# One core, one hybrid layer and a mixture-of-experts block: the conditioning rows gathered in one PSUM bank, and the order of Grams and transpositions in the RWKV pairs

## What is computed

```python
c_act = jax.nn.silu(c)
mod = c_act @ w_mod[l] + b_mod[l]
sh1, sc1, gt1, sh2, sc2, gt2 = [m[:, None, :] for m in jnp.split(mod, 6, axis=-1)]
```

```python
def step(S, inp):
    r_t, w_t, k_t, v_t, a_t, b_t = inp
    sa = jnp.einsum("bhij,bhj->bhi", S, a_t)
    S = S * w_t[:, :, None, :] + sa[..., None] * b_t[:, :, None, :] + v_t[..., None] * k_t[:, :, None, :]
    return S, jnp.einsum("bhij,bhj->bhi", S, r_t)
```

## Time and profile before

| | |
|---|---|
| median of 3 runs | 1735.11 us |
| lowest and highest | 1726.75 and 1745.92 us |
| the profiled execution | 1739.57 us |
| its span | 1737.6 us |
| TensorE busy | 1664.8 us, 96% |
| VectorE busy | 1199.7 us, 69% |
| ScalarE busy | 481.5 us, 28% |
| mean granted clock of TensorE | 0.981 of full |

### The profile page before, as it was taken

One profiled execution on the slowest core, in us unless ns is written; L12 is line 12 of the kernel. 1 busy time (PEld: TensorE's weight loads), 2 busy tenths in 40 slices (PEclk: granted clock), 3 DMA queues, 4 the chain that ended last, 5 costly groups with the idle time before them and its releaser, 6 DMA issues.

```text
span 1737.6 us, 29242 instructions
## 1 busy us (share of the span) xinstructions
PE 1664.8 (96%) x11984; PEld 1300.4 (75%) x11984; DVE 1199.7 (69%) x1604; ACT 481.5 (28%) x743; POOL 683.5 (39%) x382
## 2 busy tenths in 40 slices
PE   8999989889899999999799999999999999999998
PEld 6887667777677888888578788778788767666665
DVE  7959586756589888888777179397555526666673
ACT  4122344423220101101331122221331025444542
POOL 4765000011546667666446534346445640000000
PEclk9999899999999999999899999999999999999999
DMA  6222432130342222222222212113222246888883
GB/s 253 98 97 97 145 126 74 53 123 3 121 159 98 97 97 97 97 97 97 97 74 97 87 60 74 49 49 118 94 73 74 97 173 239 340 323 348 345 332 141
DMA packets 34070, 230.53 MB, mean 133 GB/s; under 512 B 4132, under 2 KB 4388, under 8 KB 8232
## 3 DMA queue, kind: packets, MB, share of 16 engines
q1 hardware_dynamic: 30240, 214.48, 34.1%
q10 hardware_dynamic: 2136, 10.24, 1.5%
q0 software_dynamic: 1584, 4.21, 0.7%
HBM read 220.98 MB, written 9.50 MB: 133 GB/s over the span
## 4 chain that ended last, share of the span: by engine, by line
PE 80%; DVE 10%; DMA 5%; ACT 2%; issue 2%; POOL 1%; SPq 0%; ACTq 0%; DVEq 0%; POOLq 0%
PE psum L458 78%; DMA arena<-units 4%; DVE arena L1814 2%; DVE arena L1808 2%; PE psum L462 1%; ACT arena L1390 1%; DVE arena L1811 1%; DVE expert_lo L1808 1%; ACT expert_hi L1390 1%; DMA weight_ring<-units 1%; DVE residual L1808 0%; DVE arena L2482 0%; DVE smalls L2477 0%; DVE tiny L1822 0%; DVE yb_lo L1808 0%
## 5 line engine op out<-in xcount | busy, mean ns | idle before, releaser
L1390 ACT ACTIVATE arena<-psum 128x512 f32<-128x512 f32 (+3 forms) x298 | 150.3, 520 | 781.4 <-PE psum L458 704.9
L458 PE MATMUL psum<-arena 64*64 64x64 f32 (+6 forms) x2852 | 215.8, 261 | 17.1 <-DVE arena L1808 11.9
L458 PEld LDWEIGHTS psum<-arena 64*64 64x64 f32 (+4 forms) x2852 | 144.7, 147 | 74.7 <-issue 45.7
L458 PE MATMUL psum<-normed_hi,w_in_hi 128*128 128x512 f32 x488 | 193.4, 396 | 1.1 <-POOL w_in_lo L2735 0.6
L458 PE MATMUL psum<-normed_hi,w_in_lo 128*128 128x512 f32 x488 | 190.6, 391 | 0.0
L458 PE MATMUL psum<-in_lo,w_in_hi 128*128 128x512 f32 x488 | 190.2, 390 | 0.0
L1808 DVE TENSOR_TENSOR arena<-arena,psum 128x512 f32<-128x512 f32 (+2 forms) x200 | 111.5, 588 | 103.7 <-PE psum L458 71.2
L2735 POOL TENSOR_TENSOR w_ff_lo<-weight_ring,w_ff_hi 128x1024 fp32r<-128x1024 f32 x65 | 166.2, 2557 | 5.4
L1814 DVE SCALAR_TENSOR_TENSOR arena<-arena,fixed_data 128x512 f32<-128x512 f32 x138 | 159.7, 1158 | 11.7 <-DVE arena L1811 0.2
L2735 POOL TENSOR_TENSOR w_in_lo<-weight_ring,w_in_hi 128x1024 fp32r<-128x1024 f32 x61 | 154.6, 2534 | 5.1
L2733 POOL TENSOR_SCALAR w_in_hi<-weight_ring 128x1024 fp32r<-128x1024 f32 x61 | 71.4, 1170 | 174.8 <-PE psum L458 158.7
(11 more groups left out here) (293 smaller groups left out, 3625.0 us busy)
## 6 DMA issues: line engine op xcount, KB each, us to landing
weight_ring<-units SPq DMA_DIRECT2D x124, 1024.0 KB, 4.8
arena<-units SPq DMA_DIRECT2D x55, 1024.0 KB, 7.5
normed<-units SPq DMA_DIRECT2D x20, 1024.0 KB, 7.9
slots<-arena ACTq DMA_DIRECT2D x7, 516.0 KB, 8.8
arena<-slots SPq DMA_DIRECT2D x7, 516.0 KB, 5.8
fixed_data<-fixed ACTq DMA_DIRECT2D x1, 2944.0 KB, 10.7
arena<-x SPq DMA_DIRECT2D x4, 512.0 KB, 5.9
arena<-bias_rows ACTq DMA_DIRECT2D x2, 896.0 KB, 4.5
```

Source lines behind the costliest of these rows:

```text
L458: return nc.tensor.matmul(o, l, r, start=start, stop=stop)
L1390: return nc.scalar.activation(o, i, func, **kw)
```

## The change

1. `csil` is no longer broadcast. Two regions of `tiny` (`csil_pad`) are zeroed by VectorE, and column 31 of each of their eight pieces is `csil`. A window of 32 columns that begins at 31 - i holds `csil` in its column i and zeros elsewhere. So unit i writes its sum to partition 32j + i and adds zeros to the other rows; all twenty units add into the same 256 columns of bank 7. ScalarE copies the bank once, in pair 3, TensorE turns it with two transpositions (`first_columns`), and VectorE adds the four strips (`tensor_reduce`) and then `b_mod`. The ring is freed by TensorE's last matmul of a unit.
2. In a pair the Grams `abT_crossed` and `ab` come ahead of the transpositions, which now begin with V in all pairs. VectorE masks the three Grams at once, adds the identity to X and makes the level block, and adds the identity to Z only behind it (`z_begun`, for which TensorE waits before ZU1). In pair 0 `gated(3)` follows the masks; the SSD sum uses bank 6, and its variance is inverted before the masks of `akT` and `rbT`.
3. `gt` is written alone, needing only `awa`; then `ry_r`; then `hh`, which needs `aww`. ScalarE copies in that order.

```diff
-        TM_ORDER = ((t_A, t_BP, t_KP, t_V), (t_A, t_V, t_BP, t_KP))
+        TM_ORDER = (t_V, t_A, t_BP, t_KP)
...
+        csil_pad = [tiny[:, o:o + 252].rearrange("p (k c) -> p k c", k=4) for o in (P, T + P)]
...
             def modulation(i):
 
-                if i:
-                    emptied(pe, "mod_rows", i - 1)
-                    for j in range(2):
-                        c = MOD_COLS + 2 * (i - 1) + j
-                        last = mm(PSB[7][:, c:c + 1], mod_rows[:, j * P:(j + 1) * P], sel4[:, :])
...
-                rows_of_unit(i, W_MOD_UNIT + i, 7)
+                if i == 0:
+                    pe.wait_ge(sem("csil_padded"), 1)
+                    open_("mod_all", 0, 7)
+                u = W_MOD_UNIT + i
+                pe.wait_ge(sem(f"weights{u % RING}_loaded"), 16 * (u // RING + 1))
+                w = ring[:, u % RING, :].rearrange("p (k c) -> p k c", k=KT)
+                for r in range(2):
+                    for j in range(4):
+                        k = 2 * j + r
+                        last = mm(PSB[7][32 * j:32 * j + 32, 0:256], csil_pad[k // 4][:, k % 4, 31 - i:63 - i], w[:, k, :],
+                                  i == 0 and r == 0, i == N_MOD1 - 1 and r == 1)
+                if i < N_MOD1 - 1:
+                    last.then_inc(sem("mod_unit_used"), 1)
+                else:
+                    close(last, "mod_all")
+
+            def first_columns():
+
+                emptied(pe, "mod_all")
+                o = open_("first_columns", 0, 7)
+                for h in range(2):
+                    last = tr(o[:, h * P:(h + 1) * P], mod_rows[:, h * P:(h + 1) * P])
+                close(last, "first_columns")
...
                 gram("abT", m, (5, 6), ew(e_BH), ew(e_AT))
-                for i in TM_ORDER[min(m, 1)]:
+                gram("abT_crossed", m, (0, 1), ew(e_BH), ew(e_AT), True)
+                gram("ab", m, (2, 3), ew(e_AT), ew(e_BH), True)
+                for i in TM_ORDER:
...
-                gram("abT_crossed", m, (0, 1), ew(e_BH), ew(e_AT), True)
-                gram("ab", m, (2, 3), ew(e_AT), ew(e_BH), True)
                 if m == 0:
-                    ssd_sums(1, 7)
+                    ssd_sums(1, 6)
...
+                        if lv == 1 and e == 0:
+                            pe.wait_ge(sem("z_begun"), m + 1)
...
-            modulation(N_MOD1)
+            first_columns()
...
-                if t == 1:
-                    pe.wait_ge(sem("mod_added"), 1)
...
+                    if m == 3 and lv == 4:
+                        evac("mod_all", 0, mod_rows, PSB[7][:, 0:256])
...
+                evac("ry_r", m, proj(RR + m))
                 evac("hh", m, h_all[:, :, 2 * m:2 * m + 2, :].rearrange("p t e i -> p e t i"),
                      PSB[bank_of("hh", m)].rearrange("p (e t i) -> p e t i", e=2, t=NT))
-                evac("ry_r", m, proj(RR + m))
...
+            dve.wait_ge(sem("csil_ready"), 1)
+            for half_ in csil_pad:
+                link(V.memset(half_, 0.0))
+            for i, half_ in enumerate(csil_pad):
+                last = V.tensor_copy(half_[:, :, 31:32], csil[:, 4 * i:4 * i + 4].unsqueeze(2))
+            last.then_inc(sem("csil_padded"), 1)
...
-                masked_gram("abT_crossed", m, r_AT, k_strict)
-                for e in range(2):
-                    emptied(dve, ("abT", m), e)
-                link(tt(c8(r_Z), c8(r_Z), rep8(k_ident), ALU.add))
-                masked_gram("ab", m, r_X, k_level0t)
...
                 link(tt(c8(r_X), c8(r_X), rep8(k_ident), ALU.add))
                 tt(c8(r_LV), c8(r_AT), rep8(k_level[1]), ALU.mult).then_inc(sem("blocks_ready"), 1)
+                for e in range(2):
+                    emptied(dve, ("abT", m), e)
+                tt(c8(r_Z), c8(r_Z), rep8(k_ident), ALU.add).then_inc(sem("z_begun"), 1)
+                if m == 0:
+                    invert_variance("sum_ssd1", 1.0 / 256, 1e-6)
                 masked_gram("akT", m, r_AK, k_strict)
...
-            dve.wait_ge(sem("mod_ready"), 1)
-            tt(mod[:, 0:40], PSB[7][:, MOD_COLS:MOD_COLS + 40], S("b_mod", 0, 40), ALU.add).then_inc(sem("mod_added"), 1)
+            filled(dve, "first_columns")
+            V.tensor_reduce(mod[:, 0:40].rearrange("p (i h) -> p i h", h=2),
+                            PSB[7][:, 0:256].rearrange("p (h j i) -> p i h j", h=2, j=4)[:, 0:N_MOD1, :, :], AX.X, ALU.add)                .then_inc(freed("first_columns"), 1)
+            emptied(dve, "first_columns")
+            tt(mod[:, 0:40], mod[:, 0:40], S("b_mod", 0, 40), ALU.add).then_inc(sem("mod_added"), 1)
...
-                if before in mods:
+                if mods.get(before, N_MOD) < N_MOD1 - 1:
+                    sp.wait_ge(sem("mod_unit_used"), mods[before] + 1)
```

More of the change, by code:

```diff
@@ L837, in _ @@
                 emptied(pe, "awa", m)
[L838 to L839 removed]
+                o = open_("gt", m, 2)
                 for t in range(NT):
                     for e in range(2):
[L842 removed]
                         for i in range(2):
[L844 to L854 removed]
+                            q, b = rows_of(i), 4 * e + t
+                            last = mm(c8(o)[q, b, :], c8(r_AWA)[q, b, :], tm(t_BP)[q, t, rows_of(e)])
+                close(last, "gt", m)
                 o = open_("ry_r", m, 1)
@@ L863, in _ @@
                 close(last, "ry_r", m)
+                emptied(pe, "aww", m)
+                o = open_("hh", m, 5)
+                for t in range(NT):
+                    for e in range(2):
+                        b = 4 * e + t
+                        for step in range(2):
+                            for i in range(2):
+                                q = rows_of(i)
+                                l, r = ((tm(t_BP)[q, t, rows_of(e)], c8(r_AWW)[q, b, :]),
+                                        (tm(t_KP)[q, t, rows_of(e)], tm(t_V)[q, t, rows_of(e)]))[step]
+                                last = mm(c8(o)[rows_of(1 - i), b, :], l, r, step == 0, step == 1)
+                close(last, "hh", m)
                 o = open_("ry_w", m, 4)
@@ L1530, in _ @@
                 evac("last_decay", m, pls, PSB[bank_of("last_decay", m)][:, 0:8])
-                for t in TM_ORDER[min(m, 1)]:
+                for t in TM_ORDER:
                     evac(("tm", m), t, tm(t), four(PSB[bank_of(("tm", m), t)]))
@@ L1539, in _ @@
                             rstd()
-                    if lv in (2, 4) or (m == 3 and lv in (1, 3)):
-                        mod_row(10 + 2 * m + (lv - 1 if m == 3 else lv // 2 - 1))
+                    if m == 3 and lv == 4:
+                        evac("mod_all", 0, mod_rows, PSB[7][:, 0:256])
                     if m == 0 and lv == 2:
@@ L2851, in load_unit @@
                 before = u - RING
-                if before in mods:
+                if mods.get(before, N_MOD) < N_MOD1 - 1:
+                    sp.wait_ge(sem("mod_unit_used"), mods[before] + 1)
+                elif mods.get(before) == N_MOD1 - 1:
+                    filled(sp, "mod_all")
+                elif before in mods:
                     emptied(sp, "mod_rows", mods[before])
```

33 lines of the change are left out of this document (6 added, 27 removed).

## The result

The changed kernel takes 1719.68 us in the median of 18 runs; the kernel before, on the same chip, 1733.22 us in 18. The ratio is 0.9913, with a 95% interval of 0.9893 to 0.9933: 15 us (11.6 to 18.5) faster. The forecast was 14.0 us and 1721.1 us, the likeliest of the cases named, and "within 1%" was its side.

The account below looks back on a forecast made before the run. TensorE, busy 96% of 1737.6 us, was taken as the bound. Units 7.4, pair starts 6.0, pair 1's clock 1.0, pair 0 -0.4 and gt/hh 0 sum to 14.0: 1735.1 to 1721.1 us, range 1716 to 1727, 1706 to 1734 with scatter.

Parts of the forecast that it names:

- Heads 0 to 2, 2.2 us; heads 3 to 7, 0.7: SSD heads: removed turns gain 2.2 us early, partly at half clock, then 0.7 us where VectorE's chain sets the pace.
- the clock stays up in the first heads: Rival, SSD heads: half clock from 183.9 us vanishes with the turns; gain 20.8 us, 1714.3 us; chance 0.17.
- Twenty turns: Conditioning units: removed turns, 0.54 us each at full clock, free at most 12.5 us of TensorE; 7.4 us taken.
- the turns were filler: Rival: removing turns uncovers copy latency, so pairs and heads 3 to 7 gain nothing from it; 1726.0 us; chance 0.25.
- The end, 0.3, and the set-up, hidden: Last turn becomes two transpositions (0.25 us), gaining 0.3; set-up adds under 1 us to VectorE, hidden by its idling.
- The ring: Conditioning units' weight ring: freed earlier, by TensorE's last matmul; no unit was waited for.
- The start of pairs 1 to 3: Three Grams ahead of transpositions let the first level begin 2.0 us sooner per pair, 6.0 us in all.
- Pair 1's half clock: Pair 1: half clock after the level's wait for VectorE goes with that wait; 1.0 us gained (bounds 0 and 1.7).
- Pair 0, -0.4: Pair 0's start: all sixteen transpositions now wait behind ab, a loss of 0.4 us (bounds -1.5 and +1.0).
- gt, ry_r, hh: 0: In each pair gt starts 0.9 us sooner, but separate gt and hh lose 0.8 to 1.1 us: nothing.
- Slower: the clock falls in pair 0 and stays down: Rival: pair 0's idle time then sixteen transpositions keep a whole pair at 1.2 GHz, costing 17 us; 1738 us; chance 0.05.
- The signs of being wrong: Wrong if: half clock from 183.9 gone or over 17 us; new pair-start wait over 1 us; post-392 change over 2 us.

Follow-up runs that it names:

- e14: Changed kernel with the old turns' ScalarE copies, waits and one-column matmuls put back, results unused; 1735.37 us, ratio 1.0013 to the kernel before.
- e12: The kernel of e2 run and profiled once more: changed pairs, old conditioning units with copies and turns; 1733.82 us in one run.
- e3: Changed kernel with gt and hh interleaved again ahead of ry_r, as before; 1717.61 us, ratio 0.9921 to the kernel before.
- e7: Changed kernel with conditioning units 10 and 11 moved from pair 0's levels into its TensorE pause; 1717.50 us, ratio 0.9916 to the kernel before.
- e10: As e7, plus VectorE's skip add and norm earlier in pair 0 and the variance ahead of Z's identity; 1715.15 us, ratio 0.9900 to the kernel before.
- e11: As e10, plus gt and hh interleaved again; 1717.34 us, ratio 0.9881 to the kernel before.
- e2: Changed kernel with the conditioning units' old copies and turns put back, only the pair changes kept; 1727.66 us, ratio 0.9972 to the kernel before.
- e5: Changed kernel with the turns' 38 one-column matmuls put back, without copies or waits; 1730.59 us, ratio 0.9996 to the kernel before.
- e1: Changed kernel with only the conditioning-unit change kept, pairs, gt and hh as before; 1723.72 us, ratio 0.9951 to the kernel before.
- e8: Changed kernel with six unused 128x256 matmuls on constants in TensorE's pause in pair 0; 1719.79 us, ratio 0.9926 to the kernel before.

## Why the prediction was right, and where not

The time was right because its terms were right in sum, with some luck: pair 0 came out 1.2 us better than forecast, the turns of pairs 1 and 2 0.7 us worse. By its steps:

- *Heads 0 to 2, 2.2 us; heads 3 to 7, 0.7.* Near in size: with the clock up in both, the turns cost 2.3 us in the heads (e14 against after), for 2.9. In the profiled pair the rival "the clock stays up in the first heads" happened. From unit 0 on the heads gained 9.85 us, where that rival had 2.9 + 6.8 = 9.7, and 7.5 of them are the clock, where it had 7.6. The whole stretch shows 8.2 because after had 3.4 us of half clock ahead of the heads, which cost it 1.64. But over all runs that rival's 1714.3 us did not come: half clock fell only from 57.3 to 52.4 us, a difference of 5.0 that is not clear of the scatter (give or take 5.1). Runs of the kernel before with 60 us or more at half clock average 1738.1 us (32 of 78), those with 50 to 60 us 1730.6 and those with less 1728.5 (23 each). The profile of before, with 66 us, was one of the first kind. The step that failed is the one that took a row of one execution ("The granted clock is at its 1.2 GHz level from 183.9 to 201.0 us") as a property of the kernel, and built on it both a bound of the sum and a rival. The stretch is in all three profiles with the old units, so it is no chance of one; but these executions have 66 to 69 us at half clock, above the mean of 57.3, so how many executions have it is open.
- *Twenty turns.* Pair 0's two: 43.32 us in e12 and 42.06 in after, both with 6.8 us at half clock, so 1.3 (forecast 1.0). In pairs 1 and 2 the rival "the turns were filler" was right: 35.92 and 35.91 in e12 against 35.57 and 35.84, so 0.35 and 0.07 where I had 0.54 each. I kept the turns at level 4 whole, and they gave nearly nothing, as far as single profiles tell: those of e3, e7, e10 and e11, which have no turns either, differ by up to 0.9 us in pair 1. The wait for ScalarE at level 2 has 0.75 us in after at 313.16, against 0.42 in the earlier trace rows: in the forecast's 0.4 to 1. Pair 3's were right: from unit 16 to unit 17 are 4.50 us before and 3.98 after, 0.52 a turn.
- *The end, 0.3, and the set-up, hidden.* Two transpositions take 0.44 us where I had 0.25, and nothing waits for VectorE's reduction before the state product begins at 372.25. The set-up moved nothing: the last matmuls of the state decay start at 176.03 and 175.98 us.
- *The ring: no unit was waited for.* That was wrong: removing the turns brought TensorE to unit 2 0.85 us before its transfer. The eight profiles without copies and turns all have this wait, 0.55 to 0.85 us; before, e2, e12 and e14 have none (e5 has one a unit later). A load that nothing waited for was late as soon as its reader came earlier.
- *The start of pairs 1 to 3, 2.0 each.* Right in sum. Between e1 and e3, which differ in that only, pair 1 is 37.52 and 35.04 (2.5), pair 2 37.32 and 36.12 (1.2), and from `last_decay` to unit 16 in pair 3 are 9.52 and 7.53 (2.0): 5.7 for 6.0. The missing bit is a wait that I overlooked: "The next wait, for Z, comes 2 us after Z is done" is true, but the next wait is not Z's. The product behind the level's needs the masks of `akT` and the first of `rbT`, and these now stand behind Z's identity: 0.36 us.
- *Pair 1's half clock, 1.0.* It did not come again in after, and the pair's 3.4 us is the forecast's 3.5. That the wait for VectorE brought it is not borne out: before has the same wait of 1.86 us in pairs 2 and 3, and e1 too, and the clock stayed up behind these four.
- *Pair 0, -0.4.* The sign was wrong: +0.8 (e1 against e3), within the bounds of -1.5 to +1.0. "eight transpositions more cost 1.97" at half clock was counted on TensorE, where VectorE's chain was the limit: e8 indicates that time at half clock costs nearly nothing there.
- *gt, ry_r, hh: 0.* Right in sum (e3), but `gt` came 0.4 us sooner, not 0.9. I had not looked at the masks of `rkT`, for whose bank it waits.
- *Slower: the clock falls in pair 0 and stays down.* The drop came (from 226.4, for 6.8 us) and ended as in the earlier trace rows. e8, with full clock through sixteen transpositions in a row, speaks against transpositions as its cause here; that the Trainium skill (TensorE: Matmul & The Clock Gate, Part 4: PE-mode transpose) counts them as not busy is not borne out by that row, nor is it refuted by one profile.
- *The signs of being wrong.* By its own list the prediction fails twice. The half clock from 183.9 us is gone in the profile, and something behind 392 us changed by over 2 us (the wait of 2.85). The second sign tells nothing, since that wait comes and goes between kernels that share all of that part. The first does: a shortened stretch was assumed for the heads, and no profile with the new units has it.

## What to carry to other kernels

A helper that costs half a microsecond and runs twenty times (a copy, a wait, two tiny matmuls) can be replaced by accumulating in place with a shifted, zero-padded operand and turning once: here 8.5 us by itself (4.5 to 12.6). Put independent matmuls that feed the slow engine ahead of those that don't; then ask which of its results is needed next, since each identity or mask before it is the new wait. Before a term is built on the clock of one profile, look at how the mean clock varies over all runs of the kernel.

## What the runs showed of the hardware

The scatter of a kernel's runs is mostly time at 1.2 GHz. Over 78 runs of the kernel before it lies between 34 and 87 us, and the run's time follows it with a correlation of 0.88 and a slope of 0.4 us per us; over 17 of after 0.89 and 0.5. Half rate on 7.99 and 4.44 us for the same work would give 0.44. By each kernel's own line, at 50 us of half clock, before takes 1730.2 us and after 1718.4: of the change's gain some 12 us is at equal clock, and the rest goes with less half clock. The other figures "at equal clock" in this text use one slope for all kernels, 0.41 us per us, and 50 us; those of e1 and e2 are taken against the runs of before in their own batch. They are estimates from such lines, not measured times.

In the profiles the stretches at half clock were 3.4, 6.8, 10.2, 13.7, 17.1 or 20.5 us long. And time at half clock was nearly free where TensorE waited for another engine anyway: 6.8 us of it in pair 0 cost some 0.4 (after against e8, one profile each).
